# Four small reorderings in a two-layer hybrid decoder: first column copy, end of the mLSTM, GpSimd's share of the attention weights, last block in three pieces

## The reference

```python
def rmsnorm(x, g):
    return x * rsqrt(mean(x * x) + 1e-6) * g

for i in range(2):
    z = rmsnorm(h, norm_mix_pre[i])
    z = mlstm_mixer(z, m_w_in, m_gate_bias, m_head_norm, m_w_out) if i == 0 \
        else swa_sink_mixer(z, a_w_in, a_b_in, a_sinks, a_w_out, a_b_out)
    h = h + rmsnorm(z, norm_mix_post[i])
    z = rmsnorm(h, norm_ffn_pre[i])
    gate, val = split(z @ f_w_up[i])
    z = (silu(causal_conv3(gate) + conv_b) * val) @ f_w_down[i]
    h = h + rmsnorm(z, norm_ffn_post[i])
```

## Time and profile before

| | |
|---|---|
| median of 3 runs | 1099.3 us (1099.23 to 1100.05) |
| profiled execution | 1099.89 us, span 1098.1 us |
| TensorE matmuls in flight | 1089.4 us, 99% of the span |
| VectorE busy | 532.4 us, 48% |
| ScalarE busy | 430.7 us, 39% |
| GpSimd busy | 54.1 us, 5% |
| granted clock of TensorE | 0.999 |

### The profile page before, as it was taken

The page is one execution under the profiler, slowest core; times in us unless marked ns, Lnnn a source line. Parts: engine busy times, 40 slices in busy tenths (PEclk is TensorE's granted clock), DMA queues, the critical chain, the costliest instruction groups (busy, mean ns, idle before and its releaser), DMA issues.

```text
span 1098.1 us, 14768 instructions
## 1 busy us (share of the span) xinstructions
PE 1089.4 (99%) x5562; PEld 911.7 (83%) x5562; DVE 532.4 (48%) x797; ACT 430.7 (39%) x750; POOL 54.1 (5%) x52
## 2 busy tenths in 40 slices
PE   9999999999999999999999999999999999999997
PEld 7888888898888888888889987789888888888886
DVE  7544578644444444333366576665343434523344
ACT  6511455543232324222354277754232333422242
POOL 1000211000000000000002022300000000000000
PEclk9999999999999999999999999999999999999999
DMA  8342327223323232122372632022423232303231
GB/s 269 109 119 77 115 80 228 69 71 91 111 80 114 77 115 77 39 96 96 98 189 59 173 87 68 2 77 77 115 76 115 78 113 83 108 31 102 96 134 77
DMA packets 141764, 109.51 MB, mean 100 GB/s; under 512 B 22480, under 2 KB 127088, under 8 KB 141728
## 3 DMA queue, kind: packets, MB, share of 16 engines
q1 hardware_dynamic: 140720, 105.84, 32.6%
q0 software_dynamic: 864, 2.92, 0.9%
q10 hardware_dynamic: 144, 0.26, 0.1%
HBM read 106.87 MB, written 2.13 MB: 99 GB/s over the span
## 4 chain that ended last, share of the span: by engine, by line
PE 93%; DVE 4%; ACT 2%; issue 0%; POOL 0%; DVEq 0%; ACTq 0%; POOLq 0%
PE ps L1461 18%; PE ps L1463 17%; PE ps L1462 17%; PE ps L1712 7%; PE ps L1713 7%; PE ps L1711 7%; PE ps L1656 3%; PE ps L1658 2%; PE ps L1657 2%; PE ps L1545 1%; PE ps L1547 1%; PE ps L1546 1%; PE ps L1801 1%; PE ps L1830 1%; PE ps L1812 1%; PE ps L1489 1%
## 5 line engine op out<-in xcount | busy, mean ns | idle before, releaser
L1461 PE MATMUL ps<-act_hi,w_hi 128*128 128x512 f32 (+1 forms) x1016 | 368.0, 362 | 0.1
L1462 PE MATMUL ps<-act_lo,w_hi 128*128 128x512 f32 (+1 forms) x1016 | 366.4, 361 | 0.0
L1463 PE MATMUL ps<-act_hi,w_lo 128*128 128x512 f32 (+1 forms) x1016 | 366.4, 361 | 0.0
L1461 PEld LDWEIGHTS ps<-act_hi,w_hi 128*128 128x128 f32 x1016 | 191.7, 189 | 30.7 <-DVE w_lo L916 0.9
L1463 PEld LDWEIGHTS ps<-act_hi,w_lo 128*128 128x128 f32 x1016 | 191.8, 189 | 29.1
L1462 PEld LDWEIGHTS ps<-act_lo,w_hi 128*128 128x128 f32 x1016 | 191.8, 189 | 29.0
L1711 PE MATMUL ps<-w_hi 128*128 128x512 f32 x288 | 112.0, 389 | 0.0
L1712 PE MATMUL ps<-w_lo,w_hi 128*128 128x512 f32 x288 | 112.0, 389 | 0.0
L1713 PE MATMUL ps<-w_hi,w_lo 128*128 128x512 f32 x288 | 112.0, 389 | 0.0
L749 ACT ACTIVATE arena<-ps,vecs 128x512 f32<-128x512 f32 x44 | 34.3, 780 | 188.6 <-PE ps L1463 188.6
L1242 DVE SCALAR_TENSOR_TENSOR arena<-ps,vecs,arena 128x511 f32<-128x511 f32 x44 | 33.0, 749 | 144.5 <-ACT arena L749 144.4
(11 more groups left out here) (210 smaller groups left out, 1224.0 us busy)
## 6 DMA issues: line engine op xcount, KB each, us to landing
raw<-in_f_w_up SPq DMA_DIRECT2D x88, 512.0 KB, 4.5
raw<-in_f_w_down SPq DMA_DIRECT2D x44, 512.0 KB, 3.2
raw<-in_m_w_in SPq DMA_DIRECT2D x23, 512.0 KB, 4.4
raw<-in_m_w_out SPq DMA_DIRECT2D x8, 512.0 KB, 3.3
raw<-in_a_w_in SPq DMA_DIRECT2D x16, 256.0 KB, 4.5
raw<-in_a_w_out SPq DMA_DIRECT2D x16, 256.0 KB, 4.9
h<-in_x SPq DMA_DIRECT2D x4, 512.0 KB, 7.6
h<-in_x_turned SPq DMA_DIRECT2D x3, 512.0 KB, 8.5
```

The lines of the kernel that those rows point to most:

```text
L1461: nc.tensor.matmul(dst, uh[:, k], zh, start=(k == 0), stop=False)
L1462: nc.tensor.matmul(dst, uh[:, k], zl, start=False, stop=False)
L1463: ins = nc.tensor.matmul(dst, ul[:, k], zh, start=False, stop=(k == KT - 1))
```

## The change

Four edits, none of which changes a value of the output.

1. The copy of `g_col` is issued by ScalarE's queue, behind the first weights, and no longer by SP ahead of `x_turned`. In the gate rows the unused row 6 is no longer turned, so `gt` has three columns for each chunk and head.
2. At the end of the mLSTM `scale_heads(2)` stands behind the last two splits of `m_w_out` and the gating of chunk 1.
3. GpSimd makes the low parts of units 0 and 1 of the attention's input projection, and VectorE those of 2 and 3. ScalarE's casts of units 0 and 1 stand ahead of the norm of block 0, those of 2 and 3 where 0 and 1 stood.
4. The last block is scaled, added and stored in pieces of 512, 384 and 128 columns.

```diff
+        LAST_PIECES = [slice(0, HALF), slice(HALF, D - P), slice(D - P, D)]
 @@ sync
-            nc.sync.dma_start(g_col[:], columns[:, 0:KT]).then_inc(g_col_in, 16)
             load_turned(0, 1)
...
-                for half in range(2 if b == NB - 1 else 1):
-                    hs = slice(half * HALF, (half + 1) * HALF) if b == NB - 1 else slice(0, D)
-                    sp.wait_ge(h_done, 3 * NB + b + half + 1)
+                for n, hs in enumerate(LAST_PIECES if b == NB - 1 else [slice(0, D)]):
+                    sp.wait_ge(h_done, 3 * NB + b + n + 1)
                     nc.sync.dma_start(out[0, b * P:(b + 1) * P, hs], h[:, b, hs]).then_inc(out_done, 16)
 @@ gpsimd
-            for n in range(2, 4):
+            for n in range(2):
                 s = SLOT[G_AIN + n]
                 pool.wait_ge(w_hi_done, G_AIN + n + 1)
                 pool.wait_ge(w_lo_done, counted(G_AIN + n - 1))
 @@ scalar
             nc.scalar.dma_start(raw[:, 0, 0:HALF], m_w_in[0, 0:P, 0:HALF]).then_inc(w_first_in, 16)
+            nc.scalar.dma_start(g_col[:], columns[:, 0:KT]).then_inc(g_col_in, 16)
...
+                split_hi(G_AIN)
+                split_hi(G_AIN + 1)
                 norm_post(n, 0, 0)
                 norm_pre(n + NB, 0)
-                split_hi(G_AIN)
+                split_hi(G_AIN + 2)
                 norm_post(n + 1, 1, 2)
                 norm_hi(n + NB, 0, 0)
                 norm_pre(n + NB + 1, 1)
-                split_hi(G_AIN + 1)
+                split_hi(G_AIN + 3)
                 norm_post(n + 2, 2, 4)
                 norm_hi(n + NB + 1, 1, 2)
-                split_hi(G_AIN + 2)
                 norm_post(n + 3, 3, 6)
                 norm_pre(n + NB + 2, 2)
-                split_hi(G_AIN + 3)
                 norm_pre(n + NB + 3, 3)
 @@ vector
             finish_factors(2, 2, NB)
-            scale_heads(2)
             for k in range(6, KT):
                 split_lo(G_MOUT + k)
             for half in range(2):
                 gate_heads(1, half)
             for half in range(2):
                 gated_lo(1, half)
+            scale_heads(2)
...
-                for hs in halves:
+                for hs in LAST_PIECES:
...
                 norm_pre(n + NB, 0)
-                split_lo(G_AIN)
+                dve.wait_ge(w_lo_done, counted(G_AIN + 1))
+                split_lo(G_AIN + 2)
                 norm_post(n + 1, 1, 2)
                 norm_lo(n + NB, 0, 0)
                 norm_pre(n + NB + 1, 1)
-                split_lo(G_AIN + 1)
+                split_lo(G_AIN + 3)
...
-                if n == 3:
-                    dve.wait_ge(w_lo_done, counted(G_AIN + 3))
 @@ tensor
-                for q in range(4):
-                    o0 = (c * 4 + q) * MH
-                    ins = nc.tensor.transpose(ps[:, 0, o0:o0 + MH], rows[:, 4 + q, c * P:(c + 1) * P],
+                for q, row in enumerate((4, 5, 7)):
+                    o0 = (c * 3 + q) * MH
+                    ins = nc.tensor.transpose(ps[:, 0, o0:o0 + MH], rows[:, row, c * P:(c + 1) * P],
```

More of the change, by code:

```diff
@@ L153, in trunk @@
         hn_half = sb("hn_half", [P, MH])
-        gt = sb("gt", [P, NB, 4, MH])
+        gt = sb("gt", [P, NB, 3, MH])
         dm = sb("dm", [P, NB, MH])
@@ L461, in _ @@
             for b in range(NB):
-                for half in range(2 if b == NB - 1 else 1):
-                    hs = slice(half * HALF, (half + 1) * HALF) if b == NB - 1 else slice(0, D)
-                    sp.wait_ge(h_done, 3 * NB + b + half + 1)
+                for n, hs in enumerate(LAST_PIECES if b == NB - 1 else [slice(0, D)]):
+                    sp.wait_ge(h_done, 3 * NB + b + n + 1)
                     nc.sync.dma_start(out[0, b * P:(b + 1) * P, hs], h[:, b, hs]).then_inc(out_done, 16)
-            sp.wait_ge(out_done, 16 * (NB + 1))
+            sp.wait_ge(out_done, 16 * (NB + len(LAST_PIECES) - 1))
         @block.gpsimd
@@ L1036, in _ @@
             dve.wait_ge(tr_mm, 1)
-            link(nc.vector.tensor_copy(gt[:].rearrange("p c q h -> p (c q h)"), ps[:, 0, 0:NB * 4 * MH]))
+            link(nc.vector.tensor_copy(gt[:].rearrange("p c q h -> p (c q h)"), ps[:, 0, 0:NB * 3 * MH]))
             dve.wait_ge(dec_mm, 1)
@@ L1118, in outputs @@
                 link(nc.vector.scalar_tensor_tensor(dtmp[:], den, -1.0, den, ALU.mult, ALU.max))
-                link(nc.vector.tensor_tensor(dm[:, c], dtmp[:], gt[:, c, 3], ALU.max))
+                link(nc.vector.tensor_tensor(dm[:, c], dtmp[:], gt[:, c, 2], ALU.max))
             def head_factors(c0, c1):
```

## The result

The changed kernel takes 1101.03 us in the median of 22 runs (1100.11 to 1102.98), the kernel before 1099.48 in 22 runs beside them (1099.12 to 1100.09). The ratio is 1.0016, with a 95% interval from 1.0010 to 1.0023: slower by about 1.5 us, inside the 0.2% that I called no change, and 0.13 us above the top of my range. It also scatters three times as much: five of its runs lie at 1102.2 to 1103.0 us. The profiled execution took 1101.14 us around a span of 1099.2. In the rows of the changed kernel some lines stand one lower: 917 is the low part (916 before), 930, 931 and 944 are the steps of the norm (929, 930 and 943), 600 is ScalarE's first product (599).

The account below looks back on a forecast made before the run. TensorE's queue of matmuls was taken to bound the kernel. Terms -0.65 - 0.27 + 0 + 1.25 - 0.15 = +0.2 us, added to the median 1099.3, gave 1099.5 us, called no change; range 1097.9 to 1100.9.

Parts of the forecast that it names:

- The column: Kernel start: the first norm's column, issued behind the first weights, costs TensorE nothing: 0 us, ends 0 and +0.4.
- rival 2: End of the mLSTM and gate rows give nothing, the rest as forecast: +1.1 us, 1100.4 us; chance 0.13.
- GpSimd's units: Attention projection: gap ahead of block 3 goes (-0.5), unit 1's cast delays block 0's norm (+1.75): +1.25 us.
- End of the mLSTM and gate rows: Moving scale_heads(2) nearly closes two TensorE gaps, -0.65 us; twelve gate-row turns in place of sixteen save 0.27 us.
- Last block: Final stores: a smaller last piece, issued 0.25 us later, flows some 0.45 us less: -0.15 us, ends -0.3 and +0.25.
- The estimates of 2.6 us and of 0.44 us: Final stores, by the skill's formula: today's last piece would take 2.6 us; the smaller one flows 0.44 us less.
- The norm of block 0 under the moved product: End of the mLSTM: the moved product falls into VectorE's 1.28 us wait until 181.01, so costs nothing.
- the first (no wait at block 0): Unit 1's weights land by 560.6, its cast waits for nothing, every part gains: -1.6, 1097.7 us; chance 0.17.
- The slower one: Attention projection: unit 1 lands at 564.3 or later, the whole passes +2.2 us: 1101.5 us and more; chance 0.05.

## Why the prediction missed, point by point

I forecast +0.2 us and a range up to 1100.9; measured was +1.5 and 1101.03. Term by term:

- **The column, valued 0 (ends 0 and +0.4): the step that failed.** I wrote that the column "lands today before 4.67, so at the latest by 5.1". That carries the flight time of a copy over to another place in the queues. Behind the first weights it took 4.8 us in place of 2.8. And `x_turned`, issued 0.45 us earlier, didn't land earlier: it now shared the rate with the first weights, and both came near 5.1 us (5.04 and 5.22). I also took the loss as lateness alone; with the pause that lateness makes, 10 of 44 executions of three kernels lost up to 2 us more, and the one of them that was profiled ran its first ten matmuls at the 1.2 GHz level. Alone the part is +0.9 us in the median, most of the miss of 1.3. The range failed with it: my own upper ends, added up, give +1.85 us and 1101.15, and I stopped at 1100.9, just past rival 2.
- **GpSimd's units, +1.25: right in mechanism and size.** The Square of block 0 came 1.6 us late, the waits were 1.4 and 0.3 us, with TensorE's lateness 0.48 us larger at block 1 than at block 0, against the forecast 1.2 and 0.5, and the part alone is +1.28 us in its profile (+0.9 in medians). Both halves of the argument held: the wait ahead of block 3 vanished with the overlap of GpSimd and VectorE, and the landing of unit 1 took its place. Two different edits, of ScalarE's order and of SP's, each removed it, for over 2 us each.
- **End of the mLSTM and gate rows, -0.65 and -0.27.** Together -0.81 in the profile, -0.8 in medians, against -0.92. The gate rows took 0.85 in place of 1.10 us. VectorE came forward by 0.57 and not 0.7, since the low part starts 0.1 us behind its cast, so 0.09 us of the second gap stayed.
- **Last block, -0.15: wrong in sign, +0.1 in the profiles.** I kept the end "2.0 us behind the issue whatever the size" as a bound, and for these pieces it was nearly the truth: 1.9 for 64 KB, 2.0 for 256. It isn't so for every size: the 512 KB stores of the blocks before the last one landed 2.6 us behind their issue in the kernel before, too. The last issue came 0.24 us later (3.17 us behind the last matmul, 2.93 before) and the small size gave back 0.13, not 0.4: I had taken the whole time between two issues for flow. The estimates of 2.6 us and of 0.44 us were out of place as well: the section of the Trainium skill that they come from, *DMA: Bandwidth & Descriptors*, "Anatomy of one DMA", gives its figures for copies that GpSimd issues, and these stores are SyncE's.
- **The norm of block 0 under the moved product, 0:** VectorE's scaling of chunk 2 started at 179.18 and the norm followed at 180.52, before 181.01. Right.

The parts alone add up to +0.9 + 0.9 - 0.8 - 0.1 = +0.9 us in medians and the whole is +1.5; without the column the three others add up to +0.1 and came to +0.6. Each of these numbers is uncertain by about 1 us, so this may be nothing. One thing could have added to it: if the landing of unit 1 didn't follow TensorE, the gain of the mLSTM would be lost in the stall. In the profile with the column by SP it landed at 562.33, as before, although TensorE was 1.0 us earlier than before, and TensorE stood 2.2 us at block 0. The other profiles speak against it. With the mLSTM and the gate rows alone unit 1 landed at 561.21 us, 1.1 earlier, with TensorE 1.3 earlier. In eleven of the twelve profiles with SP's order as it was, it landed 13.3 to 13.7 us behind SP's copy of the first norm gain (issued at 549.00 us in the kernel before), and only in this one 14.5; this was also the slowest of its 11 executions, 1101.06 us. The difference stays open.

Of the rivals, the first (no wait at block 0) is what the two edits of the order made true: 1098.0 us with the column by SP, against the 1097.7 that I gave it. The slower one, unit 1 landing past 564.3, didn't occur.

The Trainium skill, *DMA: Bandwidth & Descriptors*, "Issuing engines are not separate DMA queues", says that copies started by different engines run on the same sixteen DMA engines and interleave, so that another issuer saves only issue time. This trace agrees: SP's issue of `x_turned` came 0.45 us forward and its landing went 0.46 back, from 4.58 to 5.04 us.

## What to carry to other kernels

A move of a copy from one queue to another changes what it shares the rate with and what stands ahead of it; price it by the copies that will be in flight, never by its flight time today. Small copies that something waits for go ahead of large ones. An instruction put ahead of a chain on an in-order engine brings its own wait with it: before moving a cast forward, look up when its input lands.

At the head of a kernel whose TensorE warms up on dummy work, let that work last until the first operand surely is there. In some executions the pause costs more than its length: 0.65 us of it were followed by ten matmuls that took 2 us more than at the full pace.

## What the runs showed of the hardware

- The first matmuls start 0.43 us apart at the 1.2 GHz level and 0.23 at the 2.4 GHz one, while the granted clock in the profile reads 1.00 in both. How many of them go at the lower level differs from execution to execution: none to four in the ten profiles in which TensorE stood 0.2 us or less behind its warm turns, the one with 24 turns among them (none); ten in one that had stood 0.65 us; none in two that had stood 1.0 and 1.15 us.
- GpSimd's subtraction with two operands in SBUF took 2.40 us alone, and 3.25 with VectorE's line 943 stretched from 1.28 to 2.74 beside it. In the changed kernel, without that overlap, both kept their times to 0.01 us (2.40 and 1.28).
- A store of 64 KB landed 1.9 us behind its issue, one of 192 KB 1.9 or 2.0, one of 256 KB 2.0 to 2.1, one of 512 KB 2.6.
- Two norm gains of 512 KB ahead of 256-byte pieces held unit 1 back by 2.8 us (562.3 to 559.5), from the profile in which it was latest; from the usual 13.3 to 13.7 us behind SP's first issue there it is about 1.8.
